# Up projections of the squared-ReLU MLP: one VectorE subtraction for both pieces of a weight load

## The reference

```python
D_MODEL = 2048; SEQ = 256; DEPTH = 2; D_FF = 4 * D_MODEL
...
def squared_relu_mlp(h, w_up, w_down):
    a = jnp.square(jax.nn.relu(h @ w_up))
    return a @ w_down
...
    h = rmsnorm(x, ln_mlp_g[layer])
    x = x + squared_relu_mlp(h, mlp_w_up[layer], mlp_w_down[layer])
```

## Time and profile before

| | us |
|---|---|
| median of 3 runs (lowest to highest) | 2061.72 (2061.47 to 2062.61) |
| the profiled execution | 2062.04 |
| its span | 2060.3 |
| TensorE matmul busy | 2050.5 (100%) |
| TensorE weight load busy | 1758.3 (85%) |
| VectorE busy | 1459.0 (71%) |
| ScalarE busy | 1102.9 (54%) |
| GpSimd busy | 215.5 (10%) |

### The profile page before, as it was taken

How to read it: one execution, slowest core, us unless ns; L and a number is a source line. 1 busy time by engine, 2 the same in 40 slices (tenths; PEclk the granted TensorE clock), 3 DMA queues, 4 the chain that set the end, 5 groups by cost and what they waited for, 6 DMA issues and landing times.

```text
span 2060.3 us, 26470 instructions
## 1 busy us (share of the span) xinstructions
PE 2050.5 (100%) x10488; PEld 1758.3 (85%) x10488; DVE 1459.0 (71%) x1970; ACT 1102.9 (54%) x1596; POOL 215.5 (10%) x317
## 2 busy tenths in 40 slices
PE   9999999999999999999999999999999999999999
PEld 7898888888888888888889798888888888888887
DVE  6556556567966867786697688557786796687777
ACT  6555565454644544554466676444554464454454
POOL 0000000020210120120000255001110021012010
PEclk9999999999999999999999999999999999999999
DMA  8555555585885795696575443468696588679565
GB/s 283 176 155 181 169 164 164 184 254 197 258 268 188 235 294 179 198 304 203 197 234 186 143 129 123 165 206 245 200 309 203 189 263 265 201 224 291 181 197 190
DMA packets 222195, 432.35 MB, mean 210 GB/s; under 512 B 12076, under 2 KB 26488, under 8 KB 222072
## 3 DMA queue, kind: packets, MB, share of 16 engines
q1 hardware_dynamic: 200520, 380.29, 55.5%
q0 software_dynamic: 21504, 50.34, 10.6%
q10 hardware_dynamic: 48, 0.02, 0.0%
HBM read 428.52 MB, written 2.10 MB: 209 GB/s over the span
## 4 chain that ended last, share of the span: by engine, by line
PE 98%; DVE 1%; ACT 1%; DMA 0%; issue 0%; SPq 0%; DVEq 0%; ACTq 0%
PE psum L1578 23%; PE psum L1531 14%; PE psum L1533 14%; PE psum L1532 14%; PE psum L1581 12%; PE psum L1814 5%; PE psum L1813 5%; PE psum L1812 5%; PE psum L1658 1%; PE psum L1745 1%; PE psum L1602 1%; PE psum L1722 0%; PE psum L1746 0%; DMA raw<-in_sf_w_in 0%; PE psum L1702 0%; PE psum L1703 0%
## 5 line engine op out<-in xcount | busy, mean ns | idle before, releaser
L1059 DVE TENSOR_TENSOR halves<-raw,halves 128x1024 fp32r<-128x1024 f32 (+2 forms) x736 | 852.2, 1165 | 439.6 <-ACT halves L761 435.2
L761 ACT CAST halves<-raw 128x1024 fp32r<-128x1024 f32 (+2 forms) x736 | 728.5, 1001 | 601.3 <-PE psum L1533 304.3
L1578 PE MATMUL psum<-h,halves 128*128 128x512 f32 x2048 | 489.8, 391 | 0.0
L1578 PEld LDWEIGHTS psum<-h,halves 128*128 128x128 f32 x2048 | 376.4, 188 | 72.8
L1531 PE MATMUL psum<-halves,a 128*128 128x512 f32 x828 | 325.6, 393 | 0.0
L1533 PE MATMUL psum<-halves,a 128*128 128x512 f32 x828 | 322.8, 390 | 0.0
L1532 PE MATMUL psum<-halves,a 128*128 128x512 f32 x828 | 322.5, 389 | 0.0
L1581 PEld LDWEIGHTS psum<-h,halves 128*128 128x128 f32 x2048 | 262.7, 191 | 10.0
L1581 PE MATMUL psum<-h,halves 128*128 128x256 f32 x2048 | 266.1, 283 | 0.0
L1531 PE MATMUL psum<-halves,h 128*128 128x512 f32 (+4 forms) x572 | 213.4, 373 | 0.3 <-DVE h L1130 0.3
L1533 PE MATMUL psum<-halves,h 128*128 128x512 f32 (+4 forms) x572 | 206.9, 362 | 0.0
(11 more groups left out here) (264 smaller groups left out, 2080.9 us busy)
## 6 DMA issues: line engine op xcount, KB each, us to landing
raw<-in_mlp_w_up SPq DMA_DIRECT2D x128, 1024.0 KB, 6.0
raw<-in_mlp_w_down SPq DMA_DIRECT2D x128, 1024.0 KB, 5.2
mix<-in_mlp_w_down POOLq DMA_DIRECT2D x192, 256.0 KB, 6.9
raw<-in_sf_w_in SPq DMA_DIRECT2D x41, 1024.0 KB, 5.1
raw<-in_sf_w_o SPq DMA_DIRECT2D x16, 1024.0 KB, 5.1
raw<-in_mla_w_o SPq DMA_DIRECT2D x16, 1024.0 KB, 5.1
raw<-in_mla_w_ukv SPq DMA_DIRECT2D x8, 1024.0 KB, 5.6
raw<-in_sf_w_in SPq DMA_DIRECT2D x14, 512.0 KB, 4.1
```

What stands on the lines that cost most here:

```text
L761: nc.scalar.copy(half_piece(n, 0), raw_piece(n)).then_inc(hi_done, 1)
L1059: v.tensor_tensor(half_piece(n, 1), raw_piece(n), half_piece(n, 0).bitcast(F32), ALU.subtract)\
L1578: last = mm(bank, half_piece(n, 0)[:, cols], src[:, k].rearrange("p s t -> p (s t)"), start=(k == 0), stop=(k == KT - 1))
```

## The change

In the up groups VectorE no longer makes lo for each piece as it comes. `split_lo_load(n)`, with n even, waits until hi of both pieces of the load is there, subtracts over 2 × 1024 columns in one instruction, and raises `lo_done` by 2. It is called at j = 1, 3 and 5 for the pieces that were made at j = 0 and 1, 2 and 3, 4 and 5. The fourth pair of a group, pieces 8c + 10 and 8c + 11, is made where piece 8c + 11 was made, behind L1465; the call at j = 6 is gone. Mixers and down projections keep `split_lo`.

```diff
+            def split_lo_load(n):
+
+                dve.wait_ge(hi_done, n + 2)
+                slots = slice(n % SLOTS, n % SLOTS + 2)
+                whole = raw[:, PIECES[n][1] % SLOTS].rearrange("p (s n) -> p s n", s=2)
+                v.tensor_tensor(halves[:, slots, 1], whole, halves[:, slots, 0].bitcast(F32), ALU.subtract)\
+                 .then_inc(lo_done, 2)
...
                     for j in range(7):
-                        split_lo(base + 8 * c + j + AHEAD)
+                        if j % 2:
+                            split_lo_load(base + 8 * c + j - 1 + AHEAD)
                         if c and j == 1:
                             token_sums_lo(no, c if c > 1 else 0)
...
                                            op1=ALU.mult).then_inc(y_done, 1)
-                    split_lo(base + 8 * c + 7 + AHEAD)
+                    split_lo_load(base + 8 * c + 6 + AHEAD)
                     dve.wait_ge(y_hi, up0 + c + 1)
```

## The result

The change makes the kernel slower: 2116.05 us (median, 2114.07 to 2117.01) against 2061.70 us, a ratio of 1.0262 with an interval of 1.0250 to 1.0274. The profiled execution took 2117.01 us, its span is 2115.3 us, 55.0 us longer than before. The forecast was 2118 us.

The account below looks back on a forecast made before the run. TensorE was taken to set the time, with VectorE early in the up groups. Losses of 24 × 2.10 = 50.4 and 8 × 0.76 = 6.1, together 56.5 us on 2062.04, gave 2118.5, against the median 2118; bounds 2104 to 2127, range a microsecond wider on top.

Parts of the forecast that it names:

- The operation: VectorE's 2048-column subtraction: 2.31 us, bounds 2.16 to 2.46; saves 0.05 us a pair, 6.4 us in all, off the path.
- First three pairs: First three joined pairs of an up group: ready 3.6 us after the slot frees, wanted at 5.56; cover 2 us, cost 0.
- the second wait: At a group's fifth piece (p12): starts 2.10 us late, including 0.65 from the third piece, in 24 group ends.
- First wait: At a new group's third piece (p10): 0.65 us late; after the fourth group, at piece 34, 0.76 late, eight times.
- the reaction: TensorE after VectorE's end: 0.05 us to the weight load and 0.19 for a load not under a running matmul, 0.24.
- T: Start of the first matmul of the next group; the forecast's times around a group end are counted from it.
- the round trip: ScalarE waits for VectorE's token sums before hi of p12; a fourth operation 1.08 us longer delays that hi too.
- The clock did not fall in the gaps: Rival: each second wait drops the granted clock to half rate; 36 us on top, 2155 us; 6%.
- Only the first wait: Rival: the round trip over the token sums has unseen slack, so only 21.7 us remain, 2083 us; 6%.
- The operation at twice the rate: Rival: 2048 columns take no more than 1.26 us, both waits vanish and the time stays at 2062 us; 4%.
- VectorE as the bound: Rival: TensorE follows VectorE in the up groups, so 6.4 us of fixed parts are gained, 2055 us; 2%.
- SyncE's later reloads: SyncE's queue frees p12's slot of `raw` at T + 12.99 instead of T + 11.01; needed some 14 us later; cost 0.

Follow-up runs that it names:

- the middle pairs: Against the changed kernel: only the second and third pair of a group are one operation, the others single; 2061.71 us, ratio 1.0003.
- the last run: Against the changed kernel: ScalarE's token-sum cast behind hi of p12 and p13, and the fourth pair single in its old place; 2061.59 us, ratio 1.0000.
- the run with the cast later: Against the changed kernel: ScalarE's cast of the token sums moved behind hi of p12 and p13 (c = 1 to 3); 2080.68 us, ratio 1.0091.
- three pairs: Against the changed kernel: first three pairs of a group stay one operation each, the fourth single and in its old place; 2087.26 us, ratio 1.0127.
- the fourth alone: Against the changed kernel: only the fourth pair of a group is one operation, the others single; 2080.43 us, ratio 1.0093.

## Why the prediction was right

**What bounds the kernel.** TensorE, without a wait in the up groups: the middle pairs and the last run save VectorE 5.7 and 11 us and gain nothing.

**The operation.** 2.31 us was forecast from two rows, 2.289 measured. VectorE's busy time fell by 17.8 us, not by 6.4: I had compared with two operations back to back, whose recorded time overlaps, while most pieces before stood alone with their whole 1.228 us. It lies off the path, so the sum was not touched.

**First three pairs, no cost.** Right for the second and third (middle pairs: no change). The first pair is the one that the second wait is about.

**First wait.** Forecast 0.65 us at p10 and 0.76 at piece 34. Measured: 0.55 and, as the mean of eight, 0.70. The term that was mis-sized is the reaction, 0.24 in the forecast and some 0.16 at p10. At piece 34 of the second block, weight load and matmuls:

```profile
684.70 0.19 PEld L1540 LDWEIGHTS psum<-halves,a 128*128 128x128 f32 x1 [0.81 <-DVE halves L1067]
```

```profile
683.93 0.39 PE L1542 MATMUL psum<-halves,a 128*128 128x512 f32 x1
...
684.71 0.50 PE L1540 MATMUL psum<-halves,a 128*128 128x512 f32 x1 [0.38 <-DVE halves L1067]
685.05 0.40 PE L1541 MATMUL psum<-halves,a 128*128 128x512 f32 x1
...
687.60 0.39 PE L1540 MATMUL psum<-halves,a 128*128 128x512 f32 x1
```

VectorE's operation ends at 682.37 + 2.28 = 684.65 and the weight load starts 0.05 later, as forecast; it did not run ahead of the wait. But it costs 0.11, not 0.19: the second matmul follows the first by 0.34 instead of 0.227. Unhindered, the piece would have started at 684.16, so 0.55 + 0.11 = 0.66 us are lost in its first two matmuls. The next ones stand up to 0.24 apart, and piece 35 starts at 687.60 where 684.16 + 2.72 = 686.88 was due: 0.72 us. In the other blocks it is 0.68 to 0.72.

**Second wait.** The pair was to end at T + 12.99 and ended at T + 12.96; p12 was to lose 2.10 in all and lost 2.01, the difference being the reaction and the shorter operation. That its cause is the round trip is shown by the run with the cast later, and that the wait for the pair is the other half of it by the runs with three pairs and with the fourth alone.

**The sum.** 24 × 2.01 + 8 × 0.70 = 53.8 us, and 0.35 us more at the first group end of the first block (below): 54.2 of the 55.0 us by which the span grew. Forecast 56.5. The rest lies outside the MLP blocks. The first half sum comes 0.43 us earlier than before. From the last half sum of the first layer to the first of the second it takes 382.47 us instead of 380.61, 1.86 more, of which piece 34 explains 0.70. In that stretch lies the 3.2 us wait of the mixer, and behind it the granted clock stood at 0.50 for about twice as long as before. Windows of the changed kernel, of the kernel before, and of the run with three pairs, with the columns of the earlier trace rows:

```profile
1177.00:1183.00 6.00, 5.23 (x17) 4.47 (x18) 3.67 (x6) 1.68 (x4) 0.00 (x0) 0.50 0.12 43
```

```profile
1151.00:1154.00 3.00, 3.00 (x12) 2.71 (x13) 2.18 (x4) 1.68 (x4) 0.00 (x0) 0.50 0.00 0
```

```profile
1150.00:1175.00 25.00, 21.84 (x108) 18.58 (x107) 13.73 (x25) 16.62 (x44) 1.08 (x4) 1.00 0.46 144
```

In the run with three pairs the clock did not fall behind that wait at all, and the same stretch took 379.10 us. So about a microsecond of the difference between two single executions comes from the clock in this mixer and not from the change.

**The rivals.** The clock did not fall in the gaps. First the window with the longest of them, with the columns of the earlier trace rows, then the stretch with the 28 waits of the first layer:

```profile
437.00:441.00 4.00, 2.50 (x12) 1.73 (x11) 3.20 (x4) 2.30 (x3) 0.00 (x0) 1.00 1.02 393
...
420.00:1170.00 750.00, 731.08 (x3743) 619.81 (x3743) 533.90 (x584) 379.74 (x440) 69.53 (x96) 1.00 0.70 220
```

The granted clock is 1.00 in both, and 0.998 over the run. The rule that short idles between groups of matmuls make the clock swing (the Trainium skill, page "TensorE: Matmul & The Clock Gate", section "A second HAM failure mode: psum-queue depth-cycling") does not show here with 56 gaps of up to 1.5 us. "Only the first wait" is what the run with the cast later looks like, so it was the round trip that ruled it out. The operation at twice the rate and VectorE as the bound fell with 2.289 us and the runs that did not get faster. SyncE's later reloads cost nothing visible: TensorE's waits in the MLP are the 56 for the new line, and they have nearly the same length in every block.

## What to carry to other kernels

An engine's spare time says nothing about lateness: joining two operations saves a fixed part on an engine that has time to spare, and hands the first half over later by the wait for the second input plus the time of the second half. Before joining, look for the places where the producer is held up by other work (here the end of each up group) and compare the cover there, 1.25 us, with the delay; elsewhere, with 2 us of cover, the same joining was free. And where two in-order engines wait for each other in turn, time put into one of the queues comes out of the other: behind the longer fourth operation the remainder of y started 1.00 us later against T, and ScalarE started hi of p12 1.01 us later. Moving one small cast behind the urgent ones took away the 24 longer waits.

## What was not expected of the hardware

A weight load that starts only after a wait costs 0.11 us and not its whole recorded 0.19, as the starts of the matmuls behind it show.

At the first group end of the first block the pair (p12, p13) started 0.45 us after hi of p13, and TensorE's matmuls waited 1.50 us at p12 there, against 1.14 to 1.17 at the other 23 group ends. The chain around it:

```profile
436.26 1.05 ACT halves L761
437.32 0.03 issue
437.34 0.02 DVEq L1064
437.37 0.40 issue
437.76 2.30 DVE halves L1067
```

The time lies between the wait on VectorE's queue and the start of the operation, and nothing that the trace shows was being waited for. It makes 0.35 us of the loss. It is not chance: the same 0.40 us stands ahead of this operation in the three other runs that join the first pair, and in none that does not. Its cause is open.
